# Samples' attention for four samples at a time, in four column groups of the array

## The reference, cut to what matters

```python
q_lat  = einsum('bqhd,chd->bqhc', q_nope, w_uk)                    # 16 heads x 256
s_past = einsum('bqhc,bkc->bhqk', q_lat, ckv_past) + einsum('bqhr,bkr->bhqk', q_pe, kpe_past)
s_new  = the same with ckv_new, kpe_new                            # one more column
p      = softmax(concat(s_past, s_new) * ATT_SCALE)                # 16 rows x 1025 a sample
o_lat  = p[..., :n_past] @ ckv_past + p[..., n_past:] @ ckv_new
o      = einsum('bqhc,chd->bqhd', o_lat, w_uv)                     # then x += gate * (o @ w_o)
```

## Time and profile before

| | us |
|---|---|
| median of 3 executions | 3243.22 (3240.39 to 3245.75) |
| the profiled execution | 3241.1 |
| its span | 3239.3 |
| TensorE busy in the span | 2967.7 (92%) |
| the end of the prompt's last output product | 2233.4 |
| the last addition to x of the samples' attention | 2437.87, 2.31 long |
| the first MLP product of layer 1 | 2456.30 |

### The profile page before, as it was taken

One profiled execution on the slowest core, in us unless ns is written; L12 is line 12 of the kernel. 1 busy time (PEld: TensorE's weight loads), 2 busy tenths in 40 slices (PEclk: granted clock), 3 DMA queues, 4 the chain that ended last, 5 costly groups with the idle time before them and its releaser, 6 DMA issues.

```text
span 3239.3 us, 42503 instructions
## 1 busy us (share of the span) xinstructions
PE 2967.7 (92%) x17264; PEld 2632.6 (81%) x17264; DVE 1571.1 (49%) x2042; ACT 622.0 (19%) x794; POOL 1259.9 (39%) x567
## 2 busy tenths in 40 slices
PE   5799989989999999998778999997998999999997
PEld 4688879779999999997655666665467999999996
DVE  3532424255555555555656655552116555455554
ACT  4211120241001000004333222321223000011002
POOL 3312223143544444344355454641014443544433
PEclk9788989899999999998888999997978999999998
DMA  5232323132221222121010000012211111111111
GB/s 198 105 93 79 95 76 112 58 102 85 71 89 66 71 71 84 65 69 45 23 36 23 8 23 7 23 36 56 55 48 63 46 50 41 45 52 45 45 45 61
DMA packets 86393, 199.90 MB, mean 62 GB/s; under 512 B 25018, under 2 KB 43834, under 8 KB 85470
## 3 DMA queue, kind: packets, MB, share of 16 engines
q1 hardware_dynamic: 85970, 197.45, 19.1%
q10 hardware_dynamic: 336, 1.25, 0.1%
HBM read 188.07 MB, written 10.61 MB: 61 GB/s over the span
## 4 chain that ended last, share of the span: by engine, by line
PE 85%; DVE 7%; ACT 3%; issue 2%; DMA 1%; POOL 1%; SPq 1%; DVEq 0%; POOLq 0%; ACTq 0%
PE ps L612 64%; PE ps L1746 4%; PE ps L1767 3%; PE ps L571 1%; PE ps L2068 1%; PE ps L1719 1%; PE ps L1168 1%; PE ps L2111 1%; PE ps L1160 1%; PE ps L1698 1%; PE ps L1187 1%; PE ps L593 1%; PE ps L2050 1%; PE ps L2052 1%; PE ps L1189 0%
## 5 line engine op out<-in xcount | busy, mean ns | idle before, releaser
L535 POOL TENSOR_TENSOR w_hi<-w_raw,ones 128x1024 fp32r<-128x1024 f32 x171 | 423.4, 2476 | 1336.5 <-PE ps L612 1261.5
L612 PE MATMUL ps<-hn_head_f,w_hi 128*128 128x344 f32 x2112 | 451.1, 322 | 22.2 <-DVE hn_rest_f L764 19.6
L538 POOL TENSOR_TENSOR w_lo<-w_raw,w_hi 128x1024 fp32r<-128x1024 f32 x171 | 460.8, 2695 | 13.4
L612 PE MATMUL ps<-hn_rest_f,w_hi 128*128 128x344 f32 x2112 | 448.9, 321 | 0.0
L612 PE MATMUL ps<-hn_head_f,w_lo 128*128 128x344 f32 x2112 | 447.5, 320 | 0.0
L612 PEld LDWEIGHTS ps<-hn_head_f,w_hi 128*128 128x128 f32 x2112 | 355.3, 189 | 33.5 <-issue 33.4
L612 PEld LDWEIGHTS ps<-hn_rest_f,w_hi 128*128 128x128 f32 x2112 | 357.2, 189 | 0.0
L612 PEld LDWEIGHTS ps<-hn_head_f,w_lo 128*128 128x128 f32 x2112 | 353.9, 189 | 0.0
L665 DVE SCALAR_TENSOR_TENSOR x<-ps,mod,x 128x688 f32<-128x688 f32 x208 | 194.3, 934 | 305.3 <-PE ps L612 305.3
L872 DVE TENSOR_SCALAR norm_buf_f<-a_ext,conv_w_now 128x1024 f32<-128x1024 f32 x44 | 81.9, 1860 | 312.5 <-ACT a_ext L943 305.1
L612 PE MATMUL ps<-h_head,w_hi 128*128 128x344 f32 x1056 | 224.9, 321 | 7.5 <-DVE h_rest L893 7.5
(11 more groups left out here) (388 smaller groups left out, 4797.5 us busy)
## 6 DMA issues: line engine op xcount, KB each, us to landing
w_raw<-in_w_units SPq DMA_DIRECT2D x187, 512.0 KB, 3.5
ada_raw<-in_ada_units SPq DMA_DIRECT2D x104, 512.0 KB, 4.2
ada_raw_start<-in_ada_units SPq DMA_DIRECT2D x16, 512.0 KB, 14.6
pages_ckv<-in_cache_ckv SPq DMA_DIRECT2D x64, 128.0 KB, 2.0
x<-in_x SPq DMA_DIRECT2D x8, 516.0 KB, 6.5
row_bcast<-row_scratch SPq DMA_DIRECT2D x4, 1032.0 KB, 6.1
out_y<-y_tiles SPq DMA_DIRECT2D x8, 516.0 KB, 3.0
state_s<-in_state_C SPq DMA_DIRECT2D x4, 1024.0 KB, 8.0
```

The costliest lines, as they stand in the source:

```text
L535: pool.tensor_tensor(hi[s][:, 0:n, :], raw[u % 2][:, 0:n, :], ones[:, :].unsqueeze(1).to_broadcast([P, n, P]), ALU.mult).then_inc(w_head, 1)
L538: pool.tensor_tensor(lo[s][:, 0:n, :], raw[u % 2][:, 0:n, :], hi[s][:, 0:n, :].bitcast(F32), ALU.subtract).then_inc(w_split, 1)
L612: mm = nc.tensor.matmul(out(c), w, v[:, a:b], start=(first and p_ == 0), stop=(last and p_ == 2))
```

## The change

The 8 samples are taken as two groups b of four samples s (`GS = 4`). Each sample of a group has 32 partitions of the output, so 32 columns of the array (`QUARTER[s]`), of which 16 are heads. Scores, probabilities and the latent output of four samples stand together on 128 partitions, and maximum, exponential, turn and copy are one instruction for the four. The products of the four samples stand in turn in the program. The kpe pages of four samples lie side by side and are turned together. Copies of turned keys go alternately to ScalarE and VectorE (`turned_copy`). All 64 pages have a buffer of their own; many of those lie where the weight buffers are, so SyncE issues the first page only after GpSimd's last split of the prompt's weights, and issues all 64 then. w_uk and w_uv are loaded earlier. The queries' latents are computed with w_uk as the moving side and then turned. w_o is the moving side too, 16 products of 32x512 in four column groups, whose four parts are summed by eight products with a selecting matrix. Squares of x and their sum move ahead of or into the samples' attention, and only the samples' 8 columns are left behind it.

```diff
-TPS = 4
-T_N3 = T_SAMP + NS * TPS
+GS = 4
+TURNS = [[("keys", b, s, a) for s in range(GS) for a in range(2)] + [("rotated", b)] for b in range(2)]
+SAMPLE_FILLS = [("q_latent",), ("q_turned",)] + TURNS[0] + [("scores", 0)] + TURNS[1][0:5] + [("probs", 0)] \
+    + TURNS[1][5:] + [("scores", 1), ("probs", 1)]
+TS = {name: T_SAMP + k for k, name in enumerate(SAMPLE_FILLS)}
+T_N3 = T_SAMP + len(SAMPLE_FILLS)
...
     def sp_samples(Z):
         sp = nc.sync
 
-        def load(b, j):
+        def load(b, s):
 
             for g in range(NCK):
-                page = sp.value_load(Z["pt"][0:1, bass.ds(b * NCK + g, 1)], min_val=0, max_val=t["n_phys"] - 1)
-                sp.dma_start(Z["kc"][j][:, g, :], t["cache_ckv"][bass.ds(page, 1)]
-                             .rearrange("a p c -> p (a c)")).then_inc(kv_loaded[j], 16)
-                sp.dma_start(Z["kp"][j][:, g, :], t["cache_kpe"][bass.ds(page, 1)]
-                             .rearrange("a p c -> p (a c)")).then_inc(kv_loaded[j], 16)
+                k = (GS * b + s) * NCK + g
+                page = sp.value_load(Z["pt"][0:1, k:k + 1], min_val=0, max_val=t["n_phys"] - 1)
+                sp.dma_start(Z["kc"][b][s][g // 4][:, g % 4, :], t["cache_ckv"][bass.ds(page, 1)]
+                             .rearrange("a p c -> p (a c)")).then_inc(kv_loaded[b][s], 16)
+                sp.dma_start(Z["kp"][b][:, g, s, :], t["cache_kpe"][bass.ds(page, 1)]
+                             .rearrange("a p c -> p (a c)")).then_inc(kv_loaded[b][s], 16)
 
         sp.wait_ge(smp_dve, PAIRS)
+        sp.wait_ge(ring_full, AT["keys", PAIRS - 1] + 1)
+        sp.dma_start(Z["wuk"][:, :, :], t["w_ukT"]).then_inc(samp_w, 16)
+        sp.dma_start(Z["wuv"][:, :, :], t["w_uv"]).then_inc(samp_w, 16)
+        sp.wait_ge(w_split, U_PAIR + len(SPLIT_UNITS))
         sp.dma_start(Z["pt"][:, :], t["page_table"]).then_inc(pages_in, 16)
         sp.wait_ge(pages_in, 16)
-        for j in range(2):
-            load(j, j)
+        for s in range(GS):
+            load(0, s)
         sp.wait_ge(ring_full, len(RING))
-        sp.dma_start(Z["wuk"][:, :, :], t["w_ukT"]).then_inc(samp_w, 16)
-        sp.dma_start(Z["wuv"][:, :, :], t["w_uv"]).then_inc(samp_w, 16)
-        for j in range(2, 4):
-            load(j, j)
-        with sp.Fori(1, NS // 4) as i:
-            for j in range(4):
-                sp.wait_ge(z_ol, 4 * i + j - 3)
-                load(4 * i + j, j)
-
-
...
+        for s in range(GS):
+            load(1, s)
+        fl(sp, TS["q_latent",])
+        for m in range(KT // 2):
+            sp.dma_start(wo_half[:, :, m * P:(m + 1) * P], t["ada_units"][NMOD + m]).then_inc(wo_loaded, 16)
+        fl(sp, TS["rotated", 0])
+        for m in range(KT // 2):
+            for k in range(4):
+                sp.dma_start(wo_pairs[k][:, :, m * P:(m + 1) * P], t["ada_units"][NMOD + 4 + m][:, 2 * k:2 * k + 2, :])\
+                  .then_inc(wo_loaded, 16)
+        sp.wait_ge(z_pv, 1)
...
+        def keys(b, s, a):
+            T = TS["keys", b, s, a]
+            if a == 0:
+                pe.wait_ge(kv_loaded[b][s], 16 * 2 * NCK)
+            take(T)
+            for g in range(NCK):
+                mm = pe.transpose(flat(T, P, g * P), Z["kc"][b][s][g // 4][:, g % 4, a * P:(a + 1) * P], ident[:, :])
+            mm.then_inc(full, 1)
+
+        def rotated(b):
+            T = TS["rotated", b]
+            take(T)
+            for g in range(NCK):
+                mm = pe.transpose(flat(T, P, g * P), Z["kp"][b][:, g, :, :].rearrange("p s r -> p (s r)"), ident[:, :])
+            mm.then_inc(full, 1)
+
+        def scores(b):
+            T = TS["scores", b]
+            ev(pe, T - 2)
+            ev(pe, T - 1)
+            ev(pe, TS["q_turned",])
+            pe.wait_ge(z_new, b + 1)
+            take(T)
+            q_all = Z["ql"][:, :, :, :].rearrange("p a b h -> p a (b h)")
+            for (c0, c1) in ((0, 512), (512, 1024), (1024, 1025)):
+                for a in range(2):
+                    for s in range(GS):
+                        at = (GS * b + s) * MH
+                        pe.matmul(flat(T, c1 - c0, c0)[QUARTER[s]], q_all[:, a, at:at + 32],
+                                  Z["cT"][s][:, a, c0:c1], start=(a == 0), stop=False)
+                for s in range(GS):
+                    mm = pe.matmul(flat(T, c1 - c0, c0)[QUARTER[s]], Z["qr"][QUARTER[s], :],
+                                   Z["kT"][QUARTER[s], c0:c1], start=False, stop=True)
+            mm.then_inc(full, 1)
+
+        def probs(b):
+            T = TS["probs", b]
+            ev(pe, TS["scores", b])
+            take(T)
+            for g in range(NCK):
+                pe.transpose(flat(T, P, g * P), Z["pr"][:, g * P:(g + 1) * P], ident[:, :])
+            pe.matmul(flat(T, P, SEQ)[0:NS], Z["pr"][:, SEQ:SEQ + 1].to_broadcast([P, NS]), ident[:, :],
+                      start=True, stop=True).then_inc(full, 1)
+
+        def product(b):
+            ev(pe, TS["probs", b])
+            for g in range(NCK):
+                for s in range(GS):
+                    pe.matmul(ps[QUARTER[s], 6 + b, 0:KVL], Z["prT"][:, g, QUARTER[s]],
+                              Z["kc"][b][s][g // 4][:, g % 4, :], start=(g == 0), stop=False)
+            for s in range(GS):
+                mm = pe.matmul(ps[QUARTER[s], 6 + b, 0:KVL], Z["prn"][:, QUARTER[s]], Z["ckt"][:, :],
+                               start=False, stop=True)
+            mm.then_inc(z_pv, 1)
+
+        def o_turned(b):
+            pe.wait_ge(z_ol, b + 1)
+            for a in range(2):
+                mm = pe.transpose(ps[:, 6 + b, Z_OT + a * P:Z_OT + (a + 1) * P], Z["ol"][:, a * P:(a + 1) * P],
+                                  ident[:, :])
+            mm.then_inc(z_ot, 1)
+
+        for b in range(2):
+            for name in TURNS[b]:
+                if name == TURNS[1][5]:
+                    probs(0)
+                if name[0] == "keys":
+                    keys(*name[1:])
+                else:
+                    rotated(b)
+            if b == 1:
+                product(0)
+            scores(b)
+        o_turned(0)
+        probs(1)
+        product(1)
+        pe_total_prompt(3, T_N3, B3)
+        o_turned(1)
+
+        pe.wait_ge(z_olc, 2)
         for p_ in range(8):
             for a in range(2):
-                mm = pe.matmul(ps[:, 7, p_ * 16:p_ * 16 + 16], Z["wuv"][:, a, p_ * P:(p_ + 1) * P],
+                mm = pe.matmul(ps[:, 6, p_ * 16:p_ * 16 + 16], Z["wuv"][:, a, p_ * P:(p_ + 1) * P],
                                Z["olT"][:, a, 2 * p_:2 * p_ + 2, :].rearrange("p h b -> p (h b)"),
                                start=(a == 0), stop=(a == 1))
         mm.then_inc(z_pe, 1)
         pe.wait_ge(z_dve, 2)
+        pe.wait_ge(wo_loaded, 16 * (KT // 2) * 5)
+        for half in range(2):
+            for kt in range(KT):
+                w = wo_half[:, kt, :] if half == 0 else wo_pairs[kt // 2][:, kt % 2, :]
+                mm = pe.matmul(ps[QUARTER[kt % 4], 7 - half, :], Z["at"][:, kt * NS:kt * NS + 32], w,
+                               start=(kt < 4), stop=(kt >= 4))
+            mm.then_inc(z_pe, 1)
+        pe.wait_ge(z_rows, 2)
         for m in range(KT):
-            u = NMOD + m
-            pe.wait_ge(a_loaded[u % 2], (u // 2 + 1 - 2 * G_HEAD) * 16)
-            for kt in range(KT):
-                mm = pe.matmul(ps[:, 6, m * NS:(m + 1) * NS], araw[u % 2][:, kt, :], Z["at"][:, kt, :],
-                               start=(kt == 0), stop=(kt == KT - 1))
-            mm.then_inc(a_used, 1)
+            mm = pe.matmul(ps[:, 7, m * NS:(m + 1) * NS], Z["wr"][:, m * P:(m + 1) * P], sel[:, 0:NS],
+                           start=True, stop=True)
+        mm.then_inc(z_sum, 1)
...
+        act.wait_ge(sq_used, 6 * 3 + 6)
+        for b in range(2):
+            if b:
+                fl(act, TS["scores", 0])
+            for k, name in enumerate(TURNS[b]):
+                if k % 2 == 0:
+                    turned_copy(act, name, Z)
+                if b and k == 0:
+                    exps(0)
+            if b:
+                ev(act, TS["probs", 0])
+                exps(1)
+        act.wait_ge(z_pe, 3)
+        act.activation(Z["wr"][:, 0:512], ps[:, 7, :], ACT.Copy).then_inc(z_rows, 1)
...
+        def turned_probs(b):
+            T = TS["probs", b]
+            fl(dve, T)
+            if b:
+                dve.wait_ge(z_pv, 1)
+            S.done(dve.tensor_tensor(Z["prn"][:, :].rearrange("p (s h) -> p s h", s=GS),
+                                     flat(T, P, SEQ)[0:NS].rearrange("p (s h) -> p s h", s=GS),
+                                     ident[0:NS, GS * b:GS * b + GS].unsqueeze(2).to_broadcast([NS, GS, 32]),
+                                     ALU.mult))
+            S.link(dve.reciprocal(Z["ri"][:, b:b + 1], Z["rs"][:, b:b + 1]))
+            dve.tensor_copy(Z["prT"][:, :, :].rearrange("p g h -> p (g h)"), flat(T, SEQ)).then_inc(free[T % 2], 1)
...
```

(31 more changed lines are left out.)

287 lines of the change are left out of this document (131 added, 156 removed).

## The result

The changed kernel takes 3155.7 us (3151.7 to 3159.1, 4 executions), the kernel before beside it 3241.8: a ratio of 0.9739, with a 95% interval of 0.9712 to 0.9765. Five later executions gave 3160.8 and 0.9757 (0.9739 to 0.9775). The forecast was 3164 in a range of 3152 to 3190, and the way there was the forecast's case (a). The profiled execution took 3151.7.

What follows compares the result with a forecast made beforehand. SyncE's page issue, then a short tail, was taken to bound the changed kernel. 77.1 us (addition to x) plus 1.7 (norm) make 78.8 off 3241.1, so 3162.3; the median lies 2.1 above: 3164, range 3152 to 3190.

Steps and rivals of the forecast that it cites:

- case (a): Layer's end: SyncE's page issue, then a short tail; 3164 us, own range 3155 to 3173, chance 81%.
- The bound: Layer's end: TensorE bounds it before the change; afterwards SyncE's page issue does, then a short tail.
- The pages: SyncE, behind GpSimd's last split: first page out at 2207.35, then 1.70 us a page, last page there at 2317.1.
- The tail: From the last page's landing to the addition to x: summed steps of 46.0 us, addition ending 77.1 us earlier.
- The norm: Behind the addition to x: only 8 columns left to sum, ScalarE's table load last, 1.7 us saved.
- w_o's transfer: 4 MB issued at 2315, 29 us at 145 GB/s, there by 2344; wanted at 2354, so hidden by 10 us.
- (c): Rival: w_o's transfer comes late, by up to 63 us; 3174 to 3227, say 3185; chance 5%.
- TensorE's idle time: Sign: TensorE idle for 50 us or more between 2245 and 2317, waiting for pages.
- (b): Rival: TensorE's clock stays low in the tail, which costs 21.4 us more; 3186; chance 9%.
- The sentence on transposes: Skill page's statement that transposes don't count as busy time for the clock; a reason for low clock, contradicted by two rows.
- (d): Rival: the four column groups don't overlap in products, scores and w_o; 45 us more, 3209; chance 3%.
- (e): Rival: slower than before, SyncE's issue held back; loses from 2.95 us a page, 3259 at 3.2; chance 2%.

Runs made afterwards that it cites:

- the early: Changed kernel with the page table and the pages of samples 0 and 1 issued ahead of SyncE's wait for GpSimd's last split: 3130.1 us, ratio 0.9654.
- the doubled: Changed kernel with each page number read twice, the first reading thrown away: 3193.1 us, ratio 0.9864.
- GpSimd kernels: Changed kernel with the last 16 pages (samples 6 and 7) issued by GpSimd, the other 48 by SyncE: 3138.3 us, ratio 0.9687.
- early and GpSimd: Changed kernel with samples 0 and 1's pages issued ahead of the split wait and samples 6 and 7's issued by GpSimd: 3114.9 us, ratio 0.9604.
- the serial kernel: Changed kernel with scores and products issued sample by sample, so neighbouring records share a column group: 3195.8 us, ratio 0.9866.

## Why the prediction was right, step by step

**The bound.** It said that the end would be set by SyncE's pages and a short tail. The waits show it, and the early, the doubled and the GpSimd kernels show it in both directions.

**The pages.** 1.70 us a page from two rows of the kernel before; measured 1.675, with a steady step of 1.61 and single late ones of 0.9 to 1.3 us. The first page went out 2.2 us behind the table, as forecast. The error of the term is 1.3 us of 106.9. The first page went out at 2196.1 and not at 2207.35, but the whole stage lies 11.2 us earlier too: it is 26.1 us ahead of the output product's end in both.

**The tail.** Forecast 46.0, measured 46.4. Single steps are off by up to 0.7 us, and that the errors cancel is luck:

| step | forecast | measured |
|---|---|---|
| turns of keys and kpe | 4.7 | 4.75 |
| first product | 4.2 | 4.15 |
| scores | 6.8 | 6.2 |
| maximum, exponential | 2.5 | 2.6 |
| turned probabilities | 1.8 | 2.5 |
| VectorE's copy | 1.9 | 1.7 |
| second product | 6.5 | 7.2 |
| prompt's sum | 3.4 | 3.6 |
| latent output turned and copied | 0.9 | 0.7 |
| w_uv and copies | 4.5 | 4.4 |
| w_o | 5.4 | 5.4 |
| copy, selecting, VectorE's last | 3.4 | 3.25 |

The scores were 0.6 shorter: the 24 one-column records overlap too (0.45 for 1.6), and the wide ones took 5.7 for 5.2. The turned probabilities ran at the low clock throughout (granted clock 0.50 from 2321.7 to 2323.7). The Trainium skill ("TensorE: Matmul & The Clock Gate", Part 3) gives 2.38 for three groups, by which, by the prediction's estimate, the tail would have been 4 us longer. The trace disagrees: 64 records in 3.59 us against 16 in 3.57 is 4.0 for four.

**The norm.** 1.65 for 1.7. Inside it, VectorE's two multiplications of L778 took 4.54 in the first profile and 2.36 in the second, and the small one of L783 0.23 and 2.40. The long ones are those with a split of GpSimd's beside them, which began at 2356.2 in the first (L778 at 2355.8) and at 2366.7 in the second (L778 at 2364.8, L783 at 2369.5). The way to the MLP is 14.5 us in both.

**w_o's transfer.** Mis-sized on the safe side. Twenty w_o transfers were issued from 2302.6 to 2317.4, and the groups of issues say how long one is on its way (KB each, median us to landing):

```profile
w_o_first<-in_ada_units SPq DMA_DIRECT2D x4, 512.0 KB, 6.0
w_o_second<-in_ada_units SPq DMA_DIRECT2D x12, 128.0 KB, 4.0
```

All is there by about 2322, 20 us ahead of its first product. The prediction had 29 us at 145 GB/s and a cover of 10. The 145 of before was what the products at the low clock asked for, not what the transfers can give: 4 MB in 19 us are some 220 GB/s, and with the MLP's first two units behind them the window from 2302.6 to 2322.0 has 264 GB/s at a DMA share of 0.99. The kernel with w_o as weights shows nearly the time of before with no transfer at all. Rival (c) was priced from a rate that was no limit.

**TensorE's idle time.** The prediction wanted 50 us or more between 2245 and 2317, and this sign was not met: with these 72 us shifted by the 11.2 us, TensorE is idle for 43.7. In the 82 us up to the last page it is idle for 46.4, 40.0 of them waiting for pages. For the stretch between sample 3's pages and the last page the prediction's 25 us of work were about right (22.6 us busy from 2250.9 to 2304.0, at a mean granted clock of 0.66); in the 82 us it is 35.6 at 0.69, since most samples' turns begin behind a pause (16 turns in up to 3.7 us, not 2.2). Under the pages this cost nothing. With the pages out of the way TensorE's chain is the next bound at once, as the kernel "early and GpSimd" shows: of 54 us of page time removed, 44 arrived.

**The rivals.** (b), a low clock through the tail, happened in part, in the steps where the sum of 46.0 had taken it and in the turned probabilities; the tail is 46.4 us, and at the low clock throughout it would have been 67.4. The sentence on transposes, for which two rows of before spoke against the Trainium skill's page "TensorE: Matmul & The Clock Gate" (Part 4), has one more row here: with 16 added turns in place of a pause, the eight turns behind them ran at the full clock (1.09 for 1.97, granted clock 1.00 from 2331.8 to 2335.5), so here turns kept it up. (c) did not come, since w_o was there 20 us early. (d) is excluded by the serial kernel: without overlap in scores and products the time is 3196; (e) by the pace.

**The median.** 3164 was made from a profiled execution at 3241.1 and a stage 78.8 shorter; the stage measured 80.3 shorter with the norm. The first four executions came out at 3155.7, 8.7 us below the unrounded 3164.4. Of these 1.5 are the stage and the norm, 1.4 that the kernel before was itself 3241.8 and not 3243.2 this time, and the other 5.8 are not in the stage; scatter ahead of it is large enough for them. The second set, 3160.8, is 3 us off. How close each set comes to the forecast is chance.

## What to carry to other kernels

When a stage is made short, look at who issues its transfers: a page of two transfers with an address read from a table costs the issuing engine 1.6 us here, 0.52 of it for each transfer, be it 128 KB or 16 KB. The trace of the slow kernel already shows that pace where it hides nothing. Take that pace times the count as a floor before anything else, and then move issues: earlier, wherever a buffer is free, or to a second engine that is idle. Ask also in which order the consumer takes what two issuers deliver. And don't buy back a low clock at one step before knowing what the next step gets: add up all that follows.

## What the runs showed of the hardware that was not expected

- Four column groups of 32 columns overlap by 3.9 to 4.0 (256 and 512 moving columns) and by 3.3 with one moving column, if neighbours in the program are in different groups; with neighbours in one group they do not overlap at all (3.57 us for 16 records against 3.59 for 64).
- Reading a number from SBUF into SyncE's registers and checking it costs 0.55 to 0.6 us, one issue 0.52, about what one with a fixed address took (0.51). GpSimd needs 1.73 us for the same page and leaves SyncE's pace as it is.
- Products with 128 columns of weights and 8 moving ones ran at a granted clock of 0.50 for 27 us with TensorE never idle.
- When a pause ahead of TensorE's low stretch was filled, the low stretch turned up one or two steps later: four executions of three kernels have 17.7 to 17.9 us in the same 144 records. The seven other profiles with these steps lie between 16.0 and 17.8, so the length is not fixed.
- The same TensorE work ahead of the stage ended anywhere in 15 us (2220.9 to 2235.6).
